# Compressed scores as one accumulated product over zero-padded key parts, transposed back, with their probabilities taken two pairs later

## The reference, cut to what matters

```
q_raw = q.reshape(b, N_KV_A, GROUP_A, s_len, dh) * scale
kc = compress(k_cmp, pe_k, wk1, wk2)          # 15 compressed keys for each group
vc = compress(v_cmp, pe_v, wv1, wv2)
sc = jnp.einsum('bhgtd,bhcd->bhgtc', q_raw, kc).astype(jnp.float32)
c_valid = c_end[None, :] <= t[:, None]
p_cmp = jax.nn.softmax(jnp.where(c_valid, sc, NEG), axis=-1) * c_valid.any(-1)[:, None]
o_cmp = jnp.einsum('bhgtc,bhcd->bhgtd', p_cmp, vc.astype(jnp.float32))
```

## Time and profile before

| | before |
|---|---|
| median of 3 runs | 1807.85 us (1807.81 to 1808.01) |
| the profiled execution's own time | 1807.89 us |
| its span | 1806.1 us |
| PE busy | 1799.9 us |
| DVE busy | 1100.4 us |
| ACT busy | 829.2 us |
| POOL busy | 175.5 us |

### The profile page before, as it was taken

How to read it: one execution, slowest core, us unless ns; L and a number is a source line. 1 busy time by engine, 2 the same in 40 slices (tenths; PEclk the granted TensorE clock), 3 DMA queues, 4 the chain that set the end, 5 groups by cost and what they waited for, 6 DMA issues and landing times.

```text
span 1806.1 us, 22798 instructions
## 1 busy us (share of the span) xinstructions
PE 1799.9 (100%) x8222; PEld 1489.2 (82%) x8222; DVE 1100.4 (61%) x1172; ACT 829.2 (46%) x1068; POOL 175.5 (10%) x138
## 2 busy tenths in 40 slices
PE   9999999999999999999999999999999999999998
PEld 7888888888888888888888888888888888888886
DVE  7656656776877767645564557445644584445445
ACT  7643454553545445344434443444444554444443
POOL 3320003100101010220012000210022000000000
PEclk9999999999999999999999999999999999999999
DMA  9866677556555565666666656665666667666665
GB/s 295 254 195 188 187 234 226 164 157 178 150 173 163 151 176 149 189 187 186 170 189 189 187 164 187 191 191 164 188 192 190 175 187 218 209 213 204 212 205 206
DMA packets 184264, 344.77 MB, mean 191 GB/s; under 512 B 15216, under 2 KB 19568, under 8 KB 184176
## 3 DMA queue, kind: packets, MB, share of 16 engines
q1 hardware_dynamic: 183456, 342.58, 65.0%
q10 hardware_dynamic: 720, 0.93, 0.1%
HBM read 339.27 MB, written 4.19 MB: 190 GB/s over the span
## 4 chain that ended last, share of the span: by engine, by line
PE 97%; DVE 1%; issue 1%; ACT 0%; ACTq 0%; DVEq 0%
PE acc L521 30%; PE acc L527 30%; PE acc L524 30%; PE trans L538 1%; PE acc L740 1%; PE heads L567 1%; PE trans L643 1%; PE scores L552 1%; PE scores L729 0%; DVE rot_tmp L1401 0%; ACT w_parts L853 0%; PE scores L628 0%; PE scores L627 0%; PE scores L626 0%; PE heads L662 0%
## 5 line engine op out<-in xcount | busy, mean ns | idle before, releaser
L1137 DVE TENSOR_TENSOR w_parts<-raw,w_parts 128x1024 fp32r<-128x1024 f32 x620 | 775.9, 1252 | 625.3 <-ACT w_parts L853 624.0
L853 ACT ACTIVATE w_parts<-raw 128x1024 fp32r<-128x1024 f32 x620 | 656.4, 1059 | 731.5 <-PE acc L527 718.8
L521 PE MATMUL acc<-w_parts,x_parts 128*128 128x512 f32 x2424 | 954.6, 394 | 0.1
L527 PE MATMUL acc<-w_parts,x_parts 128*128 128x512 f32 x2424 | 944.9, 390 | 0.0
L524 PE MATMUL acc<-w_parts,x_parts 128*128 128x512 f32 x2424 | 943.8, 389 | 0.0
L527 PEld LDWEIGHTS acc<-w_parts,x_parts 128*128 128x128 f32 x2424 | 455.0, 188 | 96.6
L521 PEld LDWEIGHTS acc<-w_parts,x_parts 128*128 128x128 f32 x2424 | 455.3, 188 | 91.9 <-issue 0.5
L524 PEld LDWEIGHTS acc<-w_parts,x_parts 128*128 128x128 f32 x2424 | 455.6, 188 | 91.6
L459 POOL TENSOR_TENSOR rot<-tok_a,trig 128x512 f32<-128x512 f32 x18 | 30.7, 1703 | 789.8 <-ACT tok_a L859 600.7
L1476 DVE RECIPROCAL mixed<-mixed 128x256 f32<-128x256 f32 x32 | 55.9, 1747 | 0.5
L873 ACT ACTIVATE probs<-probs,negmax 128x128 f32<-128x128 f32 (+1 forms) x80 | 34.8, 436 | 28.1 <-DVE negmax L1370 27.8
(11 more groups left out here) (209 smaller groups left out, 756.6 us busy)
## 6 DMA issues: line engine op xcount, KB each, us to landing
raw<-in_w_in SPq DMA_DIRECT2D x478, 512.0 KB, 3.6
raw<-in_w_out SPq DMA_DIRECT2D x128, 512.0 KB, 4.3
raw<-in_w SPq DMA_DIRECT2D x16, 512.0 KB, 4.6
x_tok<-in_x SPq DMA_DIRECT2D x16, 256.0 KB, 5.0
xt_raw<-in_x_t SPq DMA_DIRECT2D x7, 512.0 KB, 6.1
wpost<-in_post_w SPq DMA_DIRECT2D x8, 256.0 KB, 4.9
out<-y SPq DMA_DIRECT2D x3, 512.0 KB, 2.8
out<-y SPq DMA_DIRECT2D x5, 256.0 KB, 2.2
```

Source lines behind the costliest of these rows:

```text
L521: nc.tensor.matmul(o, stat_hi, mov_hi, start=(k == 0), stop=False)
L527: last = nc.tensor.matmul(o, stat_lo, mov_hi, start=False, stop=(k == KB - 1))
L853: nc.scalar.activation(w_hi[:, n % SPLIT_SLOTS, :, 0:width], raw[:, n % RAW_SLOTS, :, 0:width], ACT.Copy).then_inc(hi_ready, 1)
L1137: V.tensor_tensor(w_lo[:, s, :, 0:width], raw[:, n % RAW_SLOTS, :, 0:width], w_hi[:, s, :, 0:width].bitcast(F32), ALU.subtract).then_inc(l ...
```

## The change

The compressed scores are laid out differently. The keys of each group stand in a wide, zeroed array `kc_wide`: 16 columns of the high part and 16 of the low part (`kc_parts`), and zeros in the other columns. A window of 128 columns of it, moved by 32 columns for each head, is now the stationary operand, and the raw queries, split into `q_hi` and `q_lo` as well, stream past it: for each of 4 heads two fp32r matmuls of 256 columns, all added up in one bank. So the bank holds for each head 32 rows of scores, tokens along the columns. ScalarE copies it to SBUF (`scores_ct`, in the first slot of `probs`), TensorE transposes it back with two transposes at pair 5, and VectorE adds mask, high-key and low-key scores.

What follows is moved by two pairs: maximum and exponential from step 3 to step 5, normalising from step 4 to 6, the transposes of `rows_c` from pair 6 to 8, the copy to `pc_t` from step 6 to 8, the product with the values from pair 8 to 10. The splits of the rotated queries go from steps 4 and 5 to steps 5 and 6, since `q_hi` and `q_lo` hold the raw queries until pair 4. `kc_wide` is zeroed by GpSimd and filled by ScalarE and VectorE in the chunk ahead of the first group.

```
-                if n == 3:
+                if n == 4:
+                    pe.wait_ge(qraw_ready, 2 + 2 * g)
+                    for h in range(HPG):
+                        o = KC_EDGE + P * g - KC_ROWS * h
+                        keys = kc_wide[:, o:o + P]
+                        nc.tensor.matmul(scores[:, 0:SEQ], keys, q_hi[:, h, :], start=(h == 0), stop=False,
+                                         skip_group_check=True)
+                        last = nc.tensor.matmul(scores[:, 0:SEQ], keys, q_lo[:, h, :], start=False, stop=(h == HPG - 1),
+                                                skip_group_check=True)
+                    last.then_inc(scores_done, 1)
+                if n == 5:
+                    pe.wait_ge(scores_free, unit + 1)
                     pe.wait_ge(tr_free, fill + 2)
-
                     for t in range(TILES):
-                        for h in range(HPG):
-                            o = (t * HPG + h) * CMP_PAD
-                            last = nc.tensor.matmul(scores[:, o:o + CMP_PAD], qraw_t[:, h, t * P:(t + 1) * P],
-                                                    kc_t[:, bass.ds(CMP_PAD * g, CMP_PAD)], start=True, stop=True)
-                    last.then_inc(scores_done, 1)
-                if n == 6:
+                        last = nc.tensor.transpose(trans[:, t * P:(t + 1) * P], scores_ct[:, t * P:(t + 1) * P], ident)
+                    last.then_inc(tr_done, 1)
+                if n == 8:
                     pe.wait_ge(probs_ready, unit + 1)
-                    pe.wait_ge(tr_free, fill + 2)
+                    pe.wait_ge(tr_free, fill + 3)
...
+            pool.wait_ge(tr_done, FILL_KC + 1)
+            pool.wait_ge(rows_ready, 1)
+            nc.gpsimd.memset(kc_wide[:, :].bitcast(F32), 0.0).then_inc(kc_zeroed, 1)
...
                 if at == 7:
-                    take_fill(FILL_KC, kc_t[:, :], trans[:, 0:64], 0.5)
+                    act.wait_ge(tr_done, FILL_KC + 1)
+                    act.wait_ge(kc_zeroed, 1)
+                    nc.scalar.activation(kc_parts[:, :, 0, :], trans[:, 0:64].rearrange("p (g c) -> p g c", g=GROUPS),
+                                         ACT.Copy, scale=0.5).then_inc(kc_hi_ready, 1)
...
                     if at in (1, 2):
-                        take_fill(fill + at - 1, qraw_t[:, :, (at - 1) * P:at * P])
-                    if at in (4, 5):
-                        t = at - 4
+                        cols = slice((at - 1) * P, at * P)
+                        take_fill(fill + at - 1, qraw_t[:, :, cols])
+                        act.wait_ge(tr_free, fill + at)
+                        nc.scalar.activation(q_hi[:, :, cols], qraw_t[:, :, cols], ACT.Copy).then_inc(qraw_hi_ready, 1)
+                    if at == 4:
+                        act.wait_ge(scores_done, unit + 1)
+                        nc.scalar.activation(scores_ct, scores[:, 0:SEQ], ACT.Copy).then_inc(scores_free, 1)
+                    if at in (5, 6):
+                        t = at - 5
...
                     if at in (2, 3):
+                        cols = slice((at - 2) * P, (at - 1) * P)
+                        dve.wait_ge(qraw_hi_ready, at - 1 + 2 * g)
+                        V.tensor_tensor(q_lo[:, :, cols], qraw_t[:, :, cols], q_hi[:, :, cols].bitcast(F32), ALU.subtract
+                                        ).then_inc(qraw_ready, 1)
                         crossed_halves(at - 2, g, fill)
-                    if at == 3:
-                        view = scores[:, 0:TILES * HPG * CMP_PAD].rearrange("p (t h c) -> p t h c", t=TILES, h=HPG)
-                        dve.wait_ge(scores_done, unit + 1)
+                    if at == 5:
+                        view = trans[:, 0:TILES * P].rearrange("p (t h a c) -> p t h a c", t=TILES, h=HPG, a=2)
+                        dve.wait_ge(tr_done, fill + 3)
                         for t in range(TILES):
-                            last = V.tensor_tensor(probs_c[:, t, :, :], view[:, t, :, :],
+                            last = V.tensor_tensor(probs_c[:, t, :, :], view[:, t, :, 0, :],
                                                    cmp_bias[:, t, :].unsqueeze(1).broadcast_to([P, HPG, CMP_PAD]),
                                                    ALU.add)
-                        last.then_inc(scores_free, 1)
-                        dve.wait_ge(scores_free, unit + 1)
+                        last.then_inc(cmp_step, 1)
+                        dve.wait_ge(cmp_step, 7 * g + 1)
+                        V.tensor_tensor(probs_c, probs_c, view[:, :, :, 1, :], ALU.add).then_inc(tr_free, 1)
...
-                    if at in (4, 5):
-                        t = at - 4
+                    if at in (5, 6):
+                        t = at - 5
                         dve.wait_ge(q_hi_ready, 2 * g + t + 1)
...
-                    if at == 4:
+                    if at == 6:
                         dve.wait_ge(exp_done, unit + 1)
```

More of the change, by code:

```diff
@@ L48 @@
 PART_ROWS = 64
+KC_ROWS = 32
+KC_EDGE = 3 * 32
 SCALE = HEAD ** -0.5
@@ L73 @@
 FILL_KSL, FILL_HIDDEN, FILL_GATE, FILL_KW, FILL_KC, FILL_VC, FILL_A = 5, 7, 8, (9, 11), 10, 12, 13
-FILLS_A, FILLS_FINAL = 9, 2
+FILLS_A, FILLS_FINAL = 10, 2
 TILES_ROTATED = 4
@@ L180, in build @@
         assert at[0] >= vc_off + 4 * GROUPS * HEAD + 4 * TILES * HPG * P
-        kc_t, _ = sb("kc_t", [P, GROUPS * CMP_PAD])
+        kc_off = vc_off + 4 * GROUPS * HEAD + 4 * TILES * HPG * P
+        kc_wide, _ = sb("kc_wide", [P, KC_EDGE + GROUPS * P], F32R, offset=kc_off)
+        at[0] = max(at[0], kc_off + 4 * (KC_EDGE + GROUPS * P))
+        kc_parts = kc_wide[:, KC_EDGE:].rearrange("p (g a c) -> p g a c", g=GROUPS, c=CMP_PAD)
         gates, _ = sb("gates", [P, TILES, N_HEADS, 3])
@@ L292, in build @@
         heads_taken = sem("heads_taken")
+        kc_zeroed = sem("kc_zeroed")
+        kc_hi_ready = sem("kc_hi_ready")
+        qraw_hi_ready = sem("qraw_hi_ready")
+        qraw_ready = sem("qraw_ready")
         q_cos_ready = sem("q_cos_ready")
@@ L595, in attention_a @@
                     last.then_inc(tr_done, 1)
-                if n == 8:
-                    pe.wait_ge(tr_free, fill + 3)
+                if n == 10:
+                    pe.wait_ge(tr_free, fill + 4)
                     if g > 0:
@@ L996, in attention_a_frame @@
                                              ).then_inc(q_hi_ready, 1)
-                    if at == 6:
-                        act.wait_ge(tr_done, fill + 3)
+                    if at == 8:
+                        act.wait_ge(tr_done, fill + 4)
                         for h in range(2):
@@ L1340, in _ @@
                         link(V.tensor_scalar(gates[:, t, :, 0], gates[:, t, :, 0], any_cmp[:, t:t + 1], None, ALU.mult))
+                if at == 7:
+                    dve.wait_ge(kc_hi_ready, 1)
+                    V.scalar_tensor_tensor(kc_parts[:, :, 1, :], trans[:, 0:64].rearrange("p (g c) -> p g c", g=GROUPS), 0.5,
+                                           kc_parts[:, :, 0, :].bitcast(F32), ALU.mult, ALU.subtract).then_inc(tr_free, 1)
                 if at == 12:
```

22 lines of the change are left out of this document (12 added, 10 removed).

## The result

| | before | after |
|---|---|---|
| median of 8 runs each | 1807.99 us (1807.81 to 1808.2) | 1813.3 us (1812.97 to 1813.73) |
| ratio, 95% interval | | 1.0029 [1.0020, 1.0038] |
| span of the profiled execution | 1806.1 us | 1810.8 us |

What follows compares the result with a forecast made beforehand. The prediction took TensorE, busy for 1799.9 of 1806.1 us, as the bound. Per group -0.89 + 1.0 + 0.2 = +0.3, four times +1.2, gave 1807.85 + 1.2 = 1809.1 us, counted as no change; eight-in-ten range from 1805.1, a little below, to 1811.6.

Steps and rivals of the forecast that it cites:

- the prices of TensorE: TensorE's work per group: eight f32 products removed, -1.80; eight fp32r matmuls added, 0.95 (0.118 each); two transposes added, 0.22.
- 1.80 - 0.95 - 0.22 = 0.63: TensorE's work per group: f32 products removed, less new matmuls and two transposes; the removed old stall of 0.26 is separate.
- the turns of VectorE and GpSimd: Operations reading two SBUF operands and GpSimd's alternate, one whole operation each; each meeting costs VectorE about 1.14.
- the near tie: At about 352 in the first group, VectorE's split of weights starts before GpSimd's addition, first by 0.06.
- the stall at pair 6: Before the first unit of scores, TensorE waits a new 1.0 per group for VectorE's rotated `q_lo`.
- VectorE's low part ends by 317.8 ... 1.3 of cover: In the chunk ahead of the groups, the keys' low part ends before TensorE reuses the bank at 319.17: no cost.
- Further on VectorE stays about 0.7 later than before ... I take a stall of 0.2 there (bounds 0 and 0.6): At pair 11, VectorE's `pt_lo` about 0.7 later, TensorE 0.1 later, with 0.4 of slack: stall of 0.2 per group.
- -0.89 + 1.0 + 0.2: Sum per group: TensorE's work and old stall -0.89, stall at pair 6 1.0, stall at pair 11 0.2; +0.3.
- the mask addition of unit 1: VectorE in the first group: ends at 369.15, before TensorE wants the bank at 370.0, so no wait.
- The first (GpSimd wins the tie): Rival at 352: TensorE waits before the compressed scores, 355.07 to 356.25; +0.7 per group, 1810.7 in all; chance 0.2.
- the second (VectorE in time): Rival at pair 6: VectorE's chain up to 3.4 shorter, no stall left; 1805.1 in all; chance 0.2.
- The third, VectorE as the bound: Rival at pairs 8 to 11: VectorE over 0.9 later than forecast, units wait for masks; 1813.9; chance 0.1.

Runs made afterwards that it cites:

- later_alone: Kernel before with only the later normalising, transposes of `rows_c` and product with the values; scores made as before: 1807.51 us.
- no_waits_left: all_three with GpSimd's second addition of a group done on 1 column in 128: 1806.0 us.
- kclo_first: Changed kernel with VectorE's low part of the keys made ahead of, not behind, its split of weights of step 7: 1812.12 us.
- raw_split_later: later_alone plus the split of the raw queries into two parts on ScalarE and VectorE, its result unused: 1808.74 us.
- all_three: Changed kernel with the edits of kclo_first and psum_early, and ScalarE's copy to `pc_t` behind its split of weights: 1806.17 us.
- psum_early: Changed kernel with the raw queries' `q_hi` and `q_lo` made from the PSUM bank, VectorE's `q_lo` one step earlier: 1808.27 us.

## Why the prediction was wrong

**Right: the prices of TensorE.** The eight matmuls took 0.117 each (forecast 0.118). The gain can be read off where nothing waits: the second matmul of the first unit stands 16.52 after the group's start in later_alone and 15.92 in no_waits_left. These 0.60 stand for 1.80 - 0.95 - 0.22 = 0.63. It reaches the group's length only where VectorE does not hold TensorE behind that place.

**Right: the turns of VectorE and GpSimd, the near tie, and the stall at pair 6.** VectorE was first at the near tie, all the turns came in the forecast order, and the chain of some 15 us ended within 0.15 of the forecast. TensorE lost 1.07 there, for 1.0. TensorE had no wait at the transposes of the probabilities, and no wait for masks at pairs 8 to 10, as forecast.

**Wrong: "VectorE's low part ends by 317.8 ... 1.3 of cover".** It ended at 320.10. I followed the data (memset, copy, low part) and not the queue: a split of weights stands ahead of the low part, and is itself late by way of ScalarE. The memset was right in length (0.61 for 0.57), and it began 0.5 later than I had it. This was 1.3 us once, and kclo_first shows it: -1.2.

**Wrong: "Further on VectorE stays about 0.7 later than before ... I take a stall of 0.2 there (bounds 0 and 0.6)".** This is the step that carries the miss. VectorE was 1.31 later at `pt_lo`, so after the slack of 0.34 the group grew by 0.97 and not by 0.3. My sum -0.89 + 1.0 + 0.2 adds up TensorE's gain and its stalls, each where it occurs. But the group's length is set by the last place where TensorE waits for VectorE: the last column of the table is 68.14 to 68.18 in ten kernels, whatever happened at pairs 3 to 8 (in later_alone without a wait shown there, a near tie). With pair 11 as the bound, -0.89 and +1.0 don't enter as terms. In after, the group grows by how much later VectorE's `pt_lo` is, less 0.34.

Where the 1.31 comes from, the table shows in two ways. By place: VectorE reaches the first mask 0.35 *earlier* than before (17.88 for 18.23), although two raw `q_lo` are new, since the normalising (1.9) and the second tile's rotated `q_lo` (0.6) now stand behind that mask. The stretch from there is 1.66 longer (18.12 for 16.46): 1.9 and 0.6, 0.39 by a wait for ScalarE shown below, less 1.23 of idle time that VectorE had there before. By steps of the change: later_alone makes `pt_lo` 0.15 later, raw_split_later 0.45 more, and the remaining 0.71 comes with what only after has, the new product and the rotated `q_lo` one step later; no run moves the latter by itself.

And why the forecast had 0.7: it has the mask addition of unit 1 end at 369.15, 23.22 after the group's start, 1.03 later than before's 22.19. It ended at 23.52. Part of this is in the prediction's own sum: from 362.6 to 368.5 are 5.9, but the operations that it lists there come to 6.2 by its own prices, and took 6.1. Behind that, before had 0.33 of idle time in front of the next mask, which takes the 1.33 to 1.00, and after has a wait for ScalarE that before has not. The next mask and the split of weights behind it, in both timelines of the second group:

```profile
474.55 0.69 DVE L1367 TENSOR_TENSOR probs<-scores,cst 128x512 f32<-128x512 f32 x1 [0.25 <-PE scores L628]
...
475.88 1.22 DVE L1137 TENSOR_TENSOR w_parts<-raw,w_parts 128x1024 fp32r<-128x1024 f32 x1
```

```profile
477.64 0.69 DVE L1400 TENSOR_TENSOR probs<-scores,cst 128x512 f32<-128x512 f32 x1
...
479.36 1.23 DVE L1166 TENSOR_TENSOR w_parts<-raw,w_parts 128x1024 fp32r<-128x1024 f32 x1 [0.32 <-ACT w_parts L873]
```

The mask is 1.00 later in its group (26.42 for 25.42), the split 1.39 (28.14 for 26.75), so the wait, 0.32 in the record, costs 0.39: ScalarE's split stands behind the copy to `pc_t`, which the change moved to step 8. later_alone, which moves only this and what belongs to it, has the wait too (0.31). With 0.08 of idle time that before still had further on, that is the 1.31. The forecast put this wait at nothing. all_three, with the copy behind the split, has no such wait and ends `pt_lo` 0.30 sooner than psum_early.

**The rivals.** The first (GpSimd wins the tie) and the second (VectorE in time) did not occur. The third, VectorE as the bound, had the right mechanism and the wrong place: it put the loss at the masks of pairs 8 to 11 and let it begin only at 0.9 more delay. The time it gave, 1813.9, is nearest to 1813.3, and it had a chance of 0.1; that nearness is luck, since it came from 2 us of VectorE work ahead of pair 6 that did not appear. The account closes as 1.3 - 0.2 ahead of the groups and 3 x 1.0 + 0.7 in them: 4.8, for 4.7 between the spans. (In the last group `pt_lo` is 1.07 later, 35.60 for 34.53, less a slack of 0.35.)

## What to carry to other kernels

When an engine that is busy for 61% of the span works 95% of a stretch, find the last point in that stretch where the bounding engine waits for it, and the last point ahead of it where the second engine itself has to wait. Between the two, sum its work, the turns it gives to others and the idle time it can fill. Savings of the bounding engine and its single stalls in between don't enter the sum: here a stall of 1.0 per group was removed for nothing, while two subtractions, one moved into idle time and one that no longer waits for GpSimd, gave 1.2. Once the second engine waits at the first point, as in no_waits_left, more time taken from it ahead of there is worth nothing. And when an operation frees a buffer, read what stands in front of it in its queue, and what that waits for.

## What the runs showed of the hardware that was not expected

- GpSimd's addition on 128x4 elements took 1.19 in the profile beside VectorE's split, for 2.26 with 128x512 elements at the same place in after: it ends 0.08 after the end of the split that it meets, and takes nothing measurable from VectorE (two splits 2.37, as without GpSimd).
- The memset of `kc_wide` started 0.55 after the matmuls that released it had ended, in after and in kclo_first alike. The next memset of GpSimd, of `pc_t`, starts 0.06 to 0.15 after its releaser. I have no explanation.
- A dependent VectorE operation behind a reciprocal of 128x4 starts 0.34 or 0.35 after it, though the reciprocal itself takes 0.17 (477.01 and 477.35 in before, 480.50 and 480.85 in after). It is so before and after the change, and is no part of the loss.
